# Turn of branch a's rows one block later, behind the first gate block of that branch

## The reference

```python
h = x @ w_in                       # ua va za | q k v | zb | ga gb, 1024 columns each
va = layer_norm(gelu(va))
ya = gelu(ua) * (causal w_s over 128-token chunks of va, + bias) * silu(za)
q, k = rope(q) * 64 ** -0.5, rope(k)
o = softmax(q1 k1) v - lam * softmax(q2 k2) v       # causal, 8 heads
yb = rms_norm(o) * silu(zb)
merged = sigmoid(ga) * (ya @ w_branch_a) + sigmoid(gb) * (yb @ w_branch_b)
x = layer_norm(alpha * x + merged @ w_out + sigmoid(x @ w_ple_gate) * (p @ w_ple))
```

## Time and profile before

| | us |
|---|---|
| median of 3 runs | 1136.77 |
| lowest, highest | 1136.58, 1137.79 |
| the profiled execution | 1138.23 |
| its span, first to last instruction | 1136.5 |
| PE busy | 1066.9 (94%) |
| DVE, ACT, POOL busy | 552.4, 392.5, 339.2 |

### The profile page before, as it was taken

One profiled execution on the slowest core, in us unless ns is written; L12 is line 12 of the kernel. 1 busy time (PEld: TensorE's weight loads), 2 busy tenths in 40 slices (PEclk: granted clock), 3 DMA queues, 4 the chain that ended last, 5 costly groups with the idle time before them and its releaser, 6 DMA issues. The chain is left out here.

```text
span 1136.5 us, 12858 instructions
## 1 busy us (share of the span) xinstructions
PE 1066.9 (94%) x5006; PEld 708.3 (62%) x5006; DVE 552.4 (49%) x985; ACT 392.5 (35%) x677; POOL 339.2 (30%) x261
## 2 busy tenths in 40 slices
PE   6999999979999899899797999999999999999993
PEld 4887888868887788688576645353535444444442
DVE  5979766758657766764744312222222221212214
ACT  4645665446424554564323101111211111111112
POOL 1059855596685007909700000000000000000000
PEclk9999999989999899799896999999999999999997
DMA  9656653856665545454439299999999999999991
GB/s 327 212 185 220 218 189 134 331 175 225 240 225 183 181 148 185 149 186 150 176 135 400 78 394 416 412 417 417 417 418 418 418 416 417 416 417 416 419 369 38
DMA packets 93933, 320.65 MB, mean 282 GB/s; under 512 B 6288, under 2 KB 7328, under 8 KB 76976
## 3 DMA queue, kind: packets, MB, share of 16 engines
q1 hardware_dynamic: 92832, 316.07, 72.7%
q0 software_dynamic: 752, 3.22, 0.8%
q10 hardware_dynamic: 288, 0.52, 0.1%
HBM read 318.74 MB, written 1.05 MB: 281 GB/s over the span
## 5 line engine op out<-in xcount | busy, mean ns | idle before, releaser
L802 PE MATMUL ps<-hl,L 128*128 128x512 f32 (+1 forms) x1216 | 388.7, 401 | 14.0 <-DVE rlo L1602 8.5
L802 PEld LDWEIGHTS ps<-hl,L 128*128 128x128 f32 x1216 | 231.7, 193 | 64.1 <-issue 15.8
L1602 DVE TENSOR_TENSOR rlo<-ring,hl 128x1024 fp32r<-128x1024 f32 (+1 forms) x154 | 211.5, 1393 | 112.9 <-ACT hl L1236 112.5
L802 PE MATMUL ps<-rlo,L 128*128 128x512 f32 (+1 forms) x608 | 241.5, 397 | 0.0
L802 PE MATMUL ps<-slots_all,xe 128*64 128x512 f32 (+1 forms) x1056 | 226.9, 582 | 0.8 <-DVE rt L2385 0.8
L1236 ACT ACTIVATE hl<-ring 128x1024 fp32r<-128x1024 f32 (+1 forms) x154 | 158.9, 1054 | 182.0 <-PE ps L802 75.2
L763 POOL TENSOR_SCALAR ring<-ring,st 128x512 f32<-128x512 f32 x84 | 176.1, 2097 | 0.0
L791 POOL CAST two<-ident 64x128 fp32r<-64x128 f32 x64 | 19.1, 298 | 488.6 <-PE ps L802 487.1
L802 PEld LDWEIGHTS ps<-slots_all,xe 128*64 128x64 f32 x1056 | 73.9, 137 | 131.7 <-issue 128.5
L802 PEld LDWEIGHTS ps<-rlo,L 128*128 128x128 f32 x608 | 117.1, 193 | 24.8
L765 POOL TENSOR_TENSOR macc<-macc,ring 128x512 f32<-128x512 f32 x84 | 116.7, 1390 | 7.0
(11 more groups left out here) (213 smaller groups left out, 915.9 us busy)
## 6 DMA issues: line engine op xcount, KB each, us to landing
slots_all<-in_w_exp_gate SPq DMA_DIRECT2D x64, 1024.0 KB, 19.9
slots_all<-in_w_exp_up SPq DMA_DIRECT2D x64, 1024.0 KB, 15.9
slots_all<-in_w_exp_down SPq DMA_DIRECT2D x64, 1024.0 KB, 16.7
ring<-in_w_in SPq DMA_DIRECT2D x49, 1024.0 KB, 5.4
ring<-in_w_mod SPq DMA_DIRECT2D x24, 1024.0 KB, 6.2
ring<-in_w_out SPq DMA_DIRECT2D x8, 1024.0 KB, 5.2
ring<-in_w_ple_gate SPq DMA_DIRECT2D x4, 1024.0 KB, 5.1
ring<-in_w_branch_a SPq DMA_DIRECT2D x4, 1024.0 KB, 7.2
```

The source lines that it names most:

```text
L802: return e.matmul(o, l, r, start=start, stop=stop)
L1602: return e.tensor_tensor(o, a, b, op)
```

## The change

The turn of branch a's rows moves on PE, ACT and DVE from before `ga0` to between `ga0` and `ga1`. On ACT and DVE it stands behind all of `project("ga0")`. The registration of its banks moves with it. `ga1`'s read-out no longer names the head 7 scores, for which `ga0`'s has waited.

```diff
-        AFTER = {"v0": "qT", "za0": "kT", "gb1": "yaT", "ba0": "ybT", "om1": "mT2"}
+        AFTER = {"v0": "qT", "za0": "kT", "ga0": "yaT", "ba0": "ybT", "om1": "mT2"}
...
-            for name in ("gb0", "gb1"):
+            for name in ("gb0", "gb1", "ga0"):
                 project(name, L0, x_ready)
             turn("yaT", lambda m, j: UA[:, m, 128 * j:128 * j + 128], lambda m, j0: w.wait_ge(ya_set, 2))
-            for name in ("ga0", "ga1", "pg0", "pg1"):
+            for name in ("ga1", "pg0", "pg1"):
                 project(name, L0, x_ready)
...
+            project("ga0", into(GA, 0), ACT.Sigmoid, ("s", 7, 1))
             rounded("yaT")
-            for c in range(2):
-                project(f"ga{c}", into(GA, c), ACT.Sigmoid, ("s", 7, 1))
+            project("ga1", into(GA, 1), ACT.Sigmoid)
...
+            project("ga0")
             completed("yaT")
-            for name in ("ga0", "ga1"):
-                project(name)
+            project("ga1")
```

## The result

| | us |
|---|---|
| before, median of 10 runs (lowest, highest) | 1136.42 (1135.15, 1138.05) |
| after, median of 10 runs (lowest, highest) | 1132.22 (1129.23, 1134.78) |
| ratio after to before, 95% interval | 0.9961 (0.9948 to 0.9974) |
| profiled execution of after, its span | 1134.78, 1133.0 |

The change makes the kernel faster by 4.2 us, by the ratio 0.4% (0.3 to 0.5%). The forecast was 1133.8 with a gain of 3.0. The profiled execution is the slowest of the ten; against the profiled one of before (1138.23) it gains 3.45. The traces show these 3.45; the 0.75 us by which the medians lie further apart is not traced.

A forecast was written before the change was run, and what follows sets the result against it. PE, busy 94% of the span, was taken to bound the kernel. 6.4 us ahead at the end of `mod6`, less 3.4 for the clock, gave 3.0; from the median 1136.77 that made 1133.8 us, range 1131.0 to 1136.9.

The forecast's parts named there:

- The old stall: PE's waits of 1.20, 1.83 and 3.05 us at the turn of `yaT` and `mod3` all go.
- DVE's room within `ga0`: DVE does two low parts at 1.2 us each and copies `o7` by 238.7, 1.5 us in time for the turn.
- The new stop: Before `mod6`, PE idles 3.5 us, 253.0 to 256.5, for `yaT` queued behind the load of piece 72.
- The clock: Behind the new wait PE runs at its lower clock, at a price of 3.4 us, between 1.7 and 5.1.
- Does the gain last?: From `ple` on, nothing binds for up to about 3 us more, so 3.0 us reach the end.
- Rival B: Gain eaten at later places (`ple`, waits at 347 and 374), or the turn still waits: 1135.7 to 1137.2; chance 0.20.
- A: Rival: behind the one wait the clock costs only 0 to 1.7 us, gain 4.7 to 6.4, 1130.4 to 1132.1; chance 0.17.
- C: Rival: piece 72's load lands 2.7 us late, sharing engines with the next, and clock costs 5.1: 1138.2, slower; chance 0.08.

The follow-up runs named there:

- e6: The kernel before with `mod3` registered, summed and added ahead of the turn, which stays before `ga0`: 1134.62 us, ratio 0.9977.
- e2: The changed kernel with ACT's roundings and DVE's completions of `yaT` ahead of piece 72, the first of `pg0`: 1132.41 us, ratio 0.9957 to the kernel before.
- e3: The changed kernel with the first two loads of `pg0` ahead of those of `mod7`: 1140.29 us, ratio 1.0020 to the kernel before.
- e1: The changed kernel once more, unchanged, beside the others on their chip: 1133.15 us, ratio 0.9961 to the kernel before.
- e5: The kernel before with the first pair of loads of `pg0` ahead of those of `mod7`, turn unmoved: 1138.9 us, ratio 1.0018.

## Why the prediction was right

**The old stall.** Said: all three waits vanish, turn at 240.2, `mod3` 1.0. Measured 240.20 and 0.95. e6 bears out the cause as told: with another name in the bank the wait stays as long (2.94 us for 3.05), as DVE's read of it stands behind the same conversions.

**DVE's room within `ga0`.** Said: low parts of 69 and 70 at 1.2 us each, the copy of `o7` done at 238.7, 1.5 us in time. Measured: DVE comes to them 0.4 us later, the two take 3.90 us instead of 2.4, and the copy is done at 240.54, 1.8 us later than said and 0.3 behind the start of the turn. By the prediction's own measure the room was overdrawn. That no wait came was luck: PE asks for that bank only with the fourth group of transposes, which at 0.48 us a group comes at 241.6, and the prediction had not counted on it.

**The new stop.** Said: ACT converts 72 at 253.19, `mod6` at 256.5 after 3.5 us of idling. Measured 253.81, 257.10 and 4.09. The load's chain ran 0.6 us later, from GpSimd's end of `mod6` (245.90 for 245.26) on, and everything behind it kept the distances that were worked out. e2 and e3 bear out both halves: with `yaT` out of the way the same load holds `pg0`, with the load early there is no stop.

**The clock.** Taken: 3.4 us, between 1.7 and 5.1. The stretch has the length that this stands for, 6.80 us at 0.50 (e1 the same). But 1.50 us of it are the rest of the wait, and `mod6` takes 2.01 us in it from its start to that of `pg0`, the same as at 1.00. Not all short matmuls are spared so: the eight of `mod3` take 1.73 us at 0.50 in the kernel before and 0.81 at 1.00 in the changed one. The windows of `mod6` after, `mod3` before and `mod3` after:

```profile
257.10:259.11 2.01, 2.01 (x16) 2.00 (x16) 2.01 (x4) 2.01 (x4) 1.93 (x3) 0.50 1.05 388
236.36:238.09 1.73, 1.73 (x8) 1.73 (x9) 1.73 (x3) 0.00 (x0) 1.65 (x2) 0.50 0.05 9
227.65:228.46 0.81, 0.81 (x9) 0.81 (x8) 0.00 (x0) 0.81 (x2) 0.81 (x2) 1.00 0.07 28
```

Only the 3.29 us from 259.11 to 262.40 are dense work at half speed, a price of 1.65. At the start of `pg0` the kernel is ahead by 264.91 - 259.11 = 5.8 us (said: 6.4), at `mod7` by 3.87 (said: 3.0). So 1.9 went between them and not 3.4, the 1.65 of the clock and the 0.3 at piece 79. This is the term that was mis-sized: I priced the stretch as if dense work filled it, though the end of the wait and `mod6` had to stand in it.

**Does the gain last?** Said: yes. `mod7` at 283.02 (said 283.9) and branch b's turn at 303.19 have it whole, and 3.45 reach the end in the profiled runs. Rival B took about 0.4 us of it. The forecast's 3.0 came near 3.45 because the errors offset, which is luck: 0.6 less by the later load, 1.5 more by the clock's price, 0.4 less on the way. "Nothing binds for a gain of up to about 3 us more" was wrong in two places. The prediction looked at `ple0` alone; ahead of it DVE's low part of piece 79 is done at 279.70 in the kernel before and wanted by PE at 284.08, so it allows 4.4 us. The changed kernel is 4.3 us earlier there and already 0.3 late; e2 waits 0.40 and 0.29 us, e3 4.54. And of e2's 2.0 us more only 0.3 were left at 349, since the loads of `w_out` bind 30 us on.

**Rivals.** A (the clock hardly drops) fell by its name, with 6.8 us at 0.50, but its price of 0 to 1.7 us is what was measured, 1.65. The gain was below its 4.7 only because other things took 1.3 us that it hadn't counted: 6.4 - 0.6 - 1.65 - 0.3 - 0.4 = 3.45. So the forecast had the mechanism of the stop right and the price of the clock wrong, and came out nearer than A by luck. C (72 late by sharing with the load right behind it) fell: from issue to ACT's start are 7.45 us, to 7.23 before, where the next load went out much later. The descriptors of one queue being taken in the order of issue ("DMA: Bandwidth & Descriptors" of the Trainium skill, section "Queues, rings and completion order") is what this shows too.

## What to carry to other kernels

When a step is moved to give its producers room, look at what stands in their queues at the new place: a conversion that waits for a load holds all behind it, and a load's time may hang on quite another engine (here GpSimd's sum). A wait that is removed ahead of such a load pays only up to it, and making the load earlier takes the slot from another that is wanted later. Price a slow stretch by the dense work that falls into it, not by its length, and don't count on its going with the wait ahead of it (e3).

## What the runs showed of the hardware

The granted clock fell to 0.50 for 3.4 us with no wait right ahead of it, behind the sums of 16 matmuls of 128x1: behind `mod7` at 286.3 in the changed kernel (3.40 of 3.40 us busy) and at 290.4 in the one before, behind `mod6` at 265.1 in e5, at 263.1 in e6 and at 255.7 in e3. Each costs 1.7 us. The same sum does not always bring it: behind `mod6` the kernel before has full clock, as e6 has behind `mod7`. No run isolates what decides. In "TensorE: Matmul & The Clock Gate" of the Trainium skill, the section "HAM oscillation — how this bites in real kernels" names waits of PE as what brings the clock down. By that alone none of these stretches would come; the rows differ, and they decide.

DVE's low part of a piece took 1.95 us (236.31, two in 3.90) beside a busy GpSimd and 1.23 at 254.90, where GpSimd's add beside it took longer instead (2.34 for 1.29 us):

```profile
237.83 1.29 POOL L765 TENSOR_TENSOR macc<-macc,ring 128x512 f32<-128x512 f32 x1
239.11 2.54 POOL L763 TENSOR_SCALAR ring<-ring,st 128x512 f32<-128x512 f32 x1
...
254.91 2.34 POOL L765 TENSOR_TENSOR macc<-macc,ring 128x512 f32<-128x512 f32 x1
```

The Trainium skill ("SBUF — State Buffer", section "SBUF: two separate sides") says that DVE and GpSimd share a pair of ports which one of them holds for a whole instruction, and counts a DVE operation with two inputs in SBUF, as these have, among those that take it. The trace agrees, with 1.2 us for an operation of DVE alone and up to 2.33 beside GpSimd in e3. A duration taken from a row beside a resting GpSimd is too low for the same work beside a busy one.
